# A two-layer four-mixer decoder trunk on one core: norm inputs split from the residual, first blocks of a stage, norm root on two columns, mixer steps respaced, layers written out

## The chip, the core and the metric

One core of one Trainium2 chip runs the whole program. The metric is the device time of one execution in microseconds (us), lower is better. The kernel before takes 1369.31 us (median of 3 runs, 1369.11 to 1370.75).

## What is computed

Two layers run on an input x of 256 tokens by 1024 channels, all in float32. The reference, cut to the skeleton:

```python
def hybrid_layer(x, ...):
    h = x + 0.5 * swiglu(rms_norm(x, ffn1_norm), ffn1_w_in, ffn1_w_out)
    u = rms_norm(h, mix_norm)
    proj = u @ w_in          # q, k, v of two attentions, S5 input, GLA inputs, 4 x 1024 gates
    y_sb, y_s5, y_gla, y_dsa = ...      # four causal mixers, each 256 wide
    mixed = jnp.sum(sigmoid(gates) * einsum(branches, w_branch), axis=2)
    h = h + mixed @ w_out
    return h + 0.5 * swiglu(rms_norm(h, ffn2_norm), ffn2_w_in, ffn2_w_out)
```

`rms_norm` divides by the root of the mean square over the 1024 channels and multiplies by a gain per channel. `swiglu` is 1024 -> 2 x 2816 -> 1024. The four mixers are stick-breaking attention ("sb"), a diagonal complex state-space scan ("s5"), gated linear attention ("gla") and dilated window attention ("dsa").

## The kernel before

**Layout.** Activations lie transposed: the residual `hT` is 128 partitions x 8 channel tiles x 256 tokens. A product with weights is made of three matmuls that replace one in float32: `three` (L418 to L422) multiplies the rounded part `hi` of one side with `hi` and `lo` of the other, and `lo` with `hi`. So each operand is split into `hi` (a rounded copy, by ScalarE) and `lo` (the rest, a subtraction).

**Weights.** They come as a stream of blocks of 128 x 2048 values. SyncE loads block after block into a ring of three slots of `raw`. ScalarE rounds a block in two halves (`round_half`, L744), VectorE subtracts in two halves (`half_rest`, L989), TensorE uses it. A block costs TensorE 48 matmuls of 128x256. VectorE's `rest_of_weights` for block m+3 stands in its program at block m, between the other work of block m.

**Stages.** A layer is FFN 1 (33 blocks), mixer (36 blocks: 11 projections, 16 gates, 4 branches, 5 output blocks) and FFN 2 (33 blocks). All engines run in the order in which their program is written, with semaphores between them, and the two layers are a hardware loop (`Fori`) on each engine.

**Norm.** The gain is applied first and the root last. After a residual pair of tiles q is ready (`hT`, 4 pairs q = 0 to 3), VectorE multiplies it by the gain into `U` (`gain_pair`, L1000), ScalarE rounds `U` (`split_pair`, L755) and squares `hT` (`square_pair`, L759), and GpSimd subtracts for the `lo` part (`split_stream`, L1436). TensorE's first block of the stage waits for `lo` of each pair. VectorE adds the four squares (`add_squares`, L1007 to L1011), TensorE sums over partitions with a matrix of -1 (`sum_squares`, L460), behind the stage's first block, with the result on 256 token columns of all partitions; for the mixer's norm it also makes two columns with the tokens on partitions. Then in `norm`: VectorE scales (L1038), ScalarE takes logarithm and exponential for the root (L789, L790, each with a table load), and VectorE makes one Newton step (L1040 to L1043) on all 256 columns. The root is applied when a product is read from PSUM: `scale` (L1072) in the FFN, `evacuate` (L1380; L874 on ScalarE) in the mixer.

**FFN.** Two input blocks give the two halves of a hidden pair, one output block takes it. `scale`, ScalarE's SiLU (L776), `product` (L1077), `hidden_hi` (L783) and `hidden_lo` (L1082) make the hidden tiles. At the end of an FFN VectorE runs `rest_of_weights`, then for q = 0 to 3 the residual (L1130) and the gain (L1000), then `rest_of_weights`, `add_squares`, and in `last_rest` the third block of weights.

**Mixer.** Its block m is called m in the code (0 "s5u", 1 "sbq", 2 "sbk", 3 "gg", 4 "dq", 5 "dk", 6 "gqk", 7 "sbv", 8 "dv", 9 "gv", 10 "gr", from 11 on the gates). Each engine has a function `pieces(m)` with what it does for the four mixers behind block m; block 3 has 24 matmuls, the others 48. The S5 scan has 8 tiles. Tile i goes through TensorE (`s5_in`), VectorE (`s5_rotate`, L1151 to L1154), GpSimd (L1529, L1530), VectorE (`s5_scan`, L1160), GpSimd (six operations, L1537 to L1543) and TensorE (`s5_out`). VectorE's part of tile i stands at m = i + 1, TensorE's `s5_out` at m = i + 4. The first scan needs GpSimd's tables (`rotations`, made during FFN 1) and `coefficients`, which needs an exponential that ScalarE makes behind the mixer's norm (L793).

The steps of the sb attention are: scores (TensorE), softplus (ScalarE, then VectorE L1202, L1205), suffix sums (`sb_suffix`, TensorE), exponential (ScalarE L884), mask (VectorE L1210), `attend`. Heads 0 and 1 go at m = 3 and 4, heads 2 and 3 at m = 5 and 6, `attend` at m = 8. At m = 7 VectorE makes the arguments of the GLA decays (L1226, L1227, 16 instructions), ScalarE their exponentials (L893, L894), and TensorE makes `gla_scores` at m = 9.

**End.** After the last residual the kernel of before still makes gain, splits, squares and weight halves for a stage that does not come, since the loop body is the same for both layers.

## Time and profile before

| what | value |
| --- | --- |
| median of 3 runs | 1369.31 us |
| the profiled execution, its own time | 1366.64 us |
| its span, first to last instruction | 1364.8 us |
| TensorE matmul busy | 1276.4 us, 94% |
| VectorE busy | 938.4 us, 69% |
| ScalarE busy | 638.8 us, 47% |
| GpSimd busy | 391.0 us, 29% |
| mean granted TensorE clock | 0.971 of full speed |
| DMA | 224.97 MB, mean 165 GB/s |

The busy shares come from one profiled execution. Matmuls are pipelined, so "busy" counts overlapping instructions once; the rate is read from how many matmuls start in a stretch. The profiled execution is 2.67 us shorter than the median of the runs.

### The profile page before, as it was taken

How to read it: one execution, taken by the hardware profiler on the slowest of the kernel's cores; microseconds unless marked ns; L12 is line 12 of the kernel's file. 1: busy time of each engine (PE TensorE's matmuls, PEld its weight loads, DVE VectorE, ACT ScalarE, POOL GpSimd, SP SyncE). 2: the span in 40 equal slices, each digit the busy share in tenths (PEclk: the TensorE clock that was granted, in tenths of full speed). 3: DMA queues.
4: the chain of work that ended last, by engine and by line, in shares of the span. 5: the costliest groups of instructions: out<-in, count | busy, mean ns of one | idle time of the engine just before them, and what ended most of it. 6: DMA issues, size and time to landing. Idle time of an engine off the chain costs nothing. (4 is left out here: it accounts for less than half of the span.)

```text
span 1364.8 us, 26906 instructions
## 1 busy us (share of the span) xinstructions
PE 1276.4 (94%) x10296; PEld 1240.6 (91%) x10296; DVE 938.4 (69%) x1249; ACT 638.8 (47%) x871; POOL 391.0 (29%) x516
## 2 busy tenths in 40 slices
PE   6999999799999899999989999996899998999996
PEld 6999998678999799999979999985799997999996
DVE  6657767778775776555676686676888567655557
ACT  5543445445554454444454434455346444544444
POOL 1389105772001510000015880167610034000001
PEclk9999999798999899999999999998899998999998
DMA  7554544223344355455535445442243543654543
GB/s 284 215 185 156 213 164 146 93 94 125 126 184 168 142 191 196 177 182 184 184 126 189 181 155 214 155 155 93 77 143 125 191 167 135 251 182 178 179 179 114
DMA packets 31478, 224.97 MB, mean 165 GB/s; under 512 B 3616, under 2 KB 3616, under 8 KB 4384
## 3 DMA queue, kind: packets, MB, share of 16 engines
q1 hardware_dynamic: 31392, 223.84, 45.5%
q8 instruction: 52, 0.85, 0.2%
q14 instruction: 34, 0.28, 0.1%
HBM read 222.78 MB, written 1.05 MB: 164 GB/s over the span
## 5 line engine op out<-in xcount | busy, mean ns | idle before, releaser
L989 DVE TENSOR_TENSOR w_lo_t<-raw,w_hi_t 128x1024 fp32r<-128x1024 f32 x414 | 529.8, 1319 | 83.1 <-ACT w_hi_t L744 83.1
L744 ACT ACTIVATE w_hi_t<-raw 128x1024 fp32r<-128x1024 f32 x414 | 414.0, 1046 | 149.2 <-PE banks L422 146.8
L420 PE MATMUL banks<-u_hi_t,w_hi_t 128*128 128x256 f32 x1552 | 449.0, 289 | 30.9 <-DVE w_lo_t L989 13.2
L421 PE MATMUL banks<-u_lo_t,w_hi_t 128*128 128x256 f32 x1552 | 444.0, 286 | 0.0
L422 PE MATMUL banks<-u_hi_t,w_lo_t 128*128 128x256 f32 x1552 | 443.7, 286 | 0.0
L420 PEld LDWEIGHTS banks<-u_hi_t,w_hi_t 128*128 128x128 f32 x1552 | 302.8, 195 | 39.1 <-issue 19.0
L421 PEld LDWEIGHTS banks<-u_lo_t,w_hi_t 128*128 128x128 f32 x1552 | 302.9, 195 | 0.1
L422 PEld LDWEIGHTS banks<-u_hi_t,w_lo_t 128*128 128x128 f32 x1552 | 302.8, 195 | 0.0
L420 PE MATMUL banks<-b_hi_t,w_hi_t 128*128 128x256 f32 x864 | 245.1, 284 | 0.6 <-POOL b_lo_t L1436 0.6
L421 PE MATMUL banks<-b_lo_t,w_hi_t 128*128 128x256 f32 x864 | 244.5, 283 | 0.0
L422 PE MATMUL banks<-b_hi_t,w_lo_t 128*128 128x256 f32 x864 | 244.5, 283 | 0.0
L420 PE MATMUL banks<-h_hi_t,w_hi_t 128*128 128x256 f32 x640 | 183.0, 286 | 8.6 <-DVE h_lo_t L1082 8.6
L421 PE MATMUL banks<-h_lo_t,w_hi_t 128*128 128x256 f32 x640 | 182.6, 285 | 0.0
L422 PE MATMUL banks<-h_hi_t,w_lo_t 128*128 128x256 f32 x640 | 182.4, 285 | 0.0
L1436 POOL TENSOR_TENSOR u_lo_t<-U,u_hi_t 128x512 fp32r<-128x512 f32 x20 | 28.2, 1412 | 526.9 <-ACT u_hi_t L755 526.9
L776 ACT ACTIVATE sbqk<-sbqk 128x256 f32<-128x256 f32 x88 | 36.7, 417 | 280.8 <-DVE sbqk L1072 280.8
L420 PEld LDWEIGHTS banks<-b_hi_t,w_hi_t 128*128 128x128 f32 x864 | 165.9, 192 | 1.0 <-POOL b_lo_t L1436 1.0
L421 PEld LDWEIGHTS banks<-b_lo_t,w_hi_t 128*128 128x128 f32 x864 | 165.9, 192 | 0.1
L422 PEld LDWEIGHTS banks<-b_hi_t,w_lo_t 128*128 128x128 f32 x864 | 165.9, 192 | 0.0
L420 PEld LDWEIGHTS banks<-h_hi_t,w_hi_t 128*128 128x128 f32 x640 | 124.2, 194 | 9.4 <-DVE h_lo_t L1082 9.4
L422 PEld LDWEIGHTS banks<-h_hi_t,w_lo_t 128*128 128x128 f32 x640 | 124.4, 194 | 0.0
L421 PEld LDWEIGHTS banks<-h_lo_t,w_hi_t 128*128 128x128 f32 x640 | 124.3, 194 | 0.0
(218 smaller groups left out, 1415.8 us busy)
## 6 DMA issues: line engine op xcount, KB each, us to landing
raw<-weights SPq DMA_DIRECT2D x207, 1024.0 KB, 4.8
prm<-params SPq DMA_DIRECT2D x2, 1178.5 KB, 5.3
prm<-params SPq DMA_DIRECT2D x1, 1166.5 KB, 15.3
cst<-constants SPq DMA_DIRECT2D x1, 1027.0 KB, 11.5
hT<-x_t SPq DMA_DIRECT2D x2, 512.0 KB, 5.1
out_t<-hT SPq DMA_DIRECT2D x4, 256.0 KB, 2.0
prm<-params SPq DMA_DIRECT2D x1, 12.0 KB, 1.8
```

What stands on the lines that cost most here:

```text
L420: pe.matmul(o, st[0], mv[0], start=start, stop=False, skip_group_check=True)
L421: pe.matmul(o, st[0], mv[1], start=False, stop=False, skip_group_check=True)
L422: ins = pe.matmul(o, st[1], mv[0], start=False, stop=stop, skip_group_check=True)
L744: act.activation(w_hi[:, slot, a:a + HALF], raw[:, slot, a:a + HALF], ACT.Copy) \
L776: act.activation(ab[:, buf, 0, :], ab[:, buf, 0, :], ACT.Silu).then_inc(s.h_silu, 1)
L989: dve.tensor_tensor(w_lo[:, slot, a:a + HALF], raw[:, slot, a:a + HALF], w_hi[:, slot, a:a + HALF].bitcast(F32), ALU.subtract).then_inc(s. ...
L1436: pool.tensor_tensor(in_lo[where][:, 2 * q:2 * q + 2, :], U[:, 2 * q:2 * q + 2, :], in_hi[where][:, 2 * q:2 * q + 2, :].bitcast(F32), ALU. ...
```

## The change

1. **Split from the residual.** `U` is no longer used for the gain. ScalarE writes `hi` as gain times `hT` (two instructions of 128x256 for a pair, the gain as scale), VectorE writes `lo` as gain times `hT` minus `hi` (two instructions of 128x256). GpSimd has no part in it. The squares go to `U`.
2. **End of an FFN.** VectorE's residuals, its splits and the two halves of a weight block alternate.
3. **First two blocks of a stage.** `first_two` runs blocks 0 and 1 one behind the other (the order in turns is there, but switched off), with `sum_squares` between them and a new `rstd_to_row` in the middle of the second. Block 2 of the mixer has a bank of its own (`bank_of`), and does not wait for the reading of block 0.
4. **Norm root on two columns.** `sum_squares` gives 128 tokens on partitions x 2 columns. GpSimd takes the power -1/2 of these 2 columns (`root`), VectorE makes the Newton step on them, and TensorE turns them back into a row over 256 columns on all partitions, which VectorE copies from PSUM. ScalarE's logarithm, exponential and their table loads for the norms go.
5. **Mixer.** The S5 tiles stand one block later on VectorE and TensorE (m = i + 2, `s5_out` at m = i + 5). The exponential that `coefficients` needs is made in FFN 1. The sb suffix sums stand at m = 5 and 8, masks at m = 6 and 9, `attend` and `gla_scores` at m = 10; most later pieces stand one block later.
6. **Layers written out** as Python loops. All waits have constant values, and the last FFN ends with the residuals. The last three weight blocks and the last parameters are not loaded.
7. **Start.** The first weight block is loaded in two halves, between and behind the halves of x.

The diff, cut to its core:

```diff
+TURNS = [(j, q) for q in range(4) for j in range(2)]
+STRAIGHT = [(j, q) for j in range(2) for q in range(4)]
+SS_AFTER, ROW_AFTER = {True: 5, False: 3}, {True: 6, False: 5}
+def bank_of(m):
+    return 2 if m == 2 else m % 2
-        squares = [yb[:, 0, :, :], yb[:, 1, :, :], sbqk[:, 0, :, :], sbqk[:, 1, :, :]]
+        squares = [U[:, 2 * q:2 * q + 2, :] for q in range(4)]
...
             sp.dma_start(hT[:, 0:4, :], x_in[:, 0:4, :]).then_inc(s_x[0], 16)
+            sp.dma_start(raw[:, 0, 0:HALF], stream[0][:, 0:HALF]).then_inc(s_first, 16)
             sp.dma_start(hT[:, 4:8, :], x_in[:, 4:8, :]).then_inc(s_x[1], 16)
-            load(0, 0)
+            sp.dma_start(raw[:, 0, HALF:BLK], stream[0][:, HALF:BLK]).then_inc(landed[0], 16)
...
-            with pe.Fori(0, LAYERS) as layer:
+            for layer in range(LAYERS):
+                def first_two(b, bank, norm, where):
+                    in_turns = False
+                    for n, (j, q) in enumerate(TURNS if in_turns else STRAIGHT):
+                        if q == 0:
+                            block_ready(b + j)
...
+                        pe.wait_ge(s.u_lo, layer * PER.u_lo + 4 * norm + q + 1)
+                        in_part(b + j, (b + j) % 3, bank + j, where, (2 * q, 2 * q + 1))
+                        if n == SS_AFTER[in_turns]:
+                            sum_squares(norm)
+                        if n == ROW_AFTER[in_turns]:
+                            rstd_to_row(norm)
...
+                    for tt in range(2):
+                        for k in range(2):
+                            ins = single(banks[:, 7, tt:tt + 1], squares[0][:, k, tt * P:(tt + 1) * P],
+                                         c("neg_ones")[:, 0:1], tt == 0 and k == 0, k == 1)
+                def rstd_to_row(norm):
+                    pe.wait_ge(s.rstd, layer * PER.rstd + norm + 1)
+                    for tt in range(2):
+                        ins = single(banks[:, 7, T + tt * P:T + (tt + 1) * P], rstd[:, norm, tt:tt + 1].to_broadcast([P, P]),
+                                     c("ident"), tt == 0, True)
+                    ins.then_inc(s.row, 1)
...
+            def split_pair(stage, name, q, where=0):
+                act.wait_ge(s.res, 4 * stage + q + 1)
+                for kt in (2 * q, 2 * q + 1):
+                    ins = act.activation(in_hi[where][:, kt, :], hT[:, kt, :], ACT.Copy, scale=p_(name)[:, kt:kt + 1])
+                ins.then_inc(s.u_hi, 1)
...
-                def norm(n):
-                    width = T + 2 if n == 1 else T
-                    act.wait_ge(s.v, layer * PER.v + n + 1)
-                    own.link(act.activation(n_y[:, 0:width], n_v[:, 0:width], ACT.Ln))
-                    act.activation(n_y[:, 0:width], n_y[:, 0:width], ACT.Exp, scale=-0.5).then_inc(s.y0, 1)
...
+            def split_pair(stage, name, q, where=0):
+                dve.wait_ge(s.u_hi, 4 * stage + q + 1)
+                for kt in (2 * q, 2 * q + 1):
+                    ins = dve.scalar_tensor_tensor(out=in_lo[where][:, kt, :], in0=hT[:, kt, :],
+                                                   scalar=p_(name)[:, kt:kt + 1],
+                                                   in1=in_hi[where][:, kt, :].bitcast(F32),
+                                                   op0=ALU.mult, op1=ALU.subtract)
+                ins.then_inc(s.u_lo, 1)
...
+                    if last:
+                        for q in range(4):
+                            residual(q)
+                        return
+                    rest_of_weights(layer, k0 + i + 1, 0)
+                    residual(0)
+                    half_rest(layer, k0 + i + 1, 1, 0)
+                    split(0)
+                    residual(1)
+                    half_rest(layer, k0 + i + 1, 1, 1)
+                    residual(2)
+                    split(1)
+                    residual(3)
+                    split(2)
+                    split(3)
                     add_squares(layer * 3 + (1 if f == 0 else 3))
+                    rest_of_weights(layer, k0 + i + 1, 2)
...
+                def root(n):
+                    pool.wait_ge(s.v, layer * PER.v + n + 1)
+                    pool.tensor_tensor(nrm[:, 1, :], nrm[:, 0, :], const(4, (P, 2)), ALU.pow).then_inc(s.y0, 1)
```

Three places show how the instructions stand. In the rows, L numbers are lines of the kernel they belong to, and `x2` means twice in a row.

The first is VectorE at the end of FFN 1. Before:

```order
L1130 SCALAR_TENSOR_TENSOR hT<-banks,hT 128x512
L1134 ISA
L1000 TENSOR_SCALAR U<-hT,prm 128x256 x2
L1127 REGISTER_ALU
L1130 SCALAR_TENSOR_TENSOR hT<-banks,hT 128x512
...
L1000 TENSOR_SCALAR U<-hT,prm 128x256 x2
L988 REGISTER_ALU
L989 TENSOR_TENSOR w_lo_t<-raw,w_hi_t 128x1024
L988 REGISTER_ALU
L989 TENSOR_TENSOR w_lo_t<-raw,w_hi_t 128x1024
```

Now:

```order
L1184 SCALAR_TENSOR_TENSOR hT<-banks,hT 128x512
L1033 TENSOR_TENSOR w_lo_t<-raw,w_hi_t 128x1024
L1045 SCALAR_TENSOR_TENSOR u_lo_t<-hT,prm,u_hi_t 128x256 x2
L1184 SCALAR_TENSOR_TENSOR hT<-banks,hT 128x512
L1033 TENSOR_TENSOR w_lo_t<-raw,w_hi_t 128x1024
L1184 SCALAR_TENSOR_TENSOR hT<-banks,hT 128x512
L1045 SCALAR_TENSOR_TENSOR u_lo_t<-hT,prm,u_hi_t 128x256 x2
L1184 SCALAR_TENSOR_TENSOR hT<-banks,hT 128x512
L1045 SCALAR_TENSOR_TENSOR u_lo_t<-hT,prm,u_hi_t 128x256 x4
L1055 TENSOR_TENSOR U<-U 128x512
```

The two weight halves moved from behind the fourth residual to behind the first two, and the `lo` part, which GpSimd made, now stands in VectorE's order.

The second is VectorE in the mixer, at the two sb heads 0 and 1 (`attA`). Before, at m = 3, behind the scan of tile 2:

```order
L989 TENSOR_TENSOR w_lo_t<-raw,w_hi_t 128x1024
L1160 SCALAR_TENSOR_TENSOR s5x<-s5n,s5x 128x256 x2
L1201 ISA
L1202 SCALAR_TENSOR_TENSOR attA<-banks,attB 128x384
L192 REGISTER_ALU
L1205 TENSOR_TENSOR attA<-attA,cst 128x384
```

Now, at m = 4, again behind the scan of tile 2:

```order
L1225 TENSOR_TENSOR s5x<-banks,G 128x256
L1033 TENSOR_TENSOR w_lo_t<-raw,w_hi_t 128x1024 x2
L1231 SCALAR_TENSOR_TENSOR s5x<-s5n,s5x 128x256 x2
L1273 SCALAR_TENSOR_TENSOR attA<-banks,attB 128x384
L1276 TENSOR_TENSOR attA<-attA,cst 128x384
```

The heads still stand behind the scan of tile 2; both moved by one block.

The third is TensorE at the first suffix sums (`attA,cst`). Before, all this stands behind block 4:

```order
L433 MATMUL banks<-s5u,prm 128x256 x2
L433 MATMUL banks<-st,s5c 32x256 x2
L613 REGISTER_ALU
L433 MATMUL banks<-gq,prm 128x256
L563 ISA
L433 MATMUL banks<-attA,cst 128x256
L433 MATMUL banks<-attA,cst 128x128 x2
```

Now, behind block 5:

```order
L438 MATMUL banks<-w_hi_t,u_lo_t 128x256
L449 MATMUL banks<-s5u,prm 128x256 x2
L449 MATMUL banks<-st,s5c 32x256 x2
L449 MATMUL banks<-attA,cst 128x256
L449 MATMUL banks<-attA,cst 128x128 x2
```

There is one block of 48 matmuls more ahead of the wait.

## Rows read from the trace of the kernel before

**Rows 1.** The page, its head and part 1: busy us (share) xinstructions

```profile
span 1364.8 us, 26906 instructions
PE 1276.4 (94%) x10296; PEld 1240.6 (91%) x10296; DVE 938.4 (69%) x1249; ACT 638.8 (47%) x871; POOL 391.0 (29%) x516
```

**Rows 2.** Windows: stretch and its us, busy us (xinstructions), PEclk, DMA share, GB/s

```profile
100.00:150.00 50.00, 50.00 (x419) 50.00 (x418) 39.66 (x35) 21.63 (x30) 37.95 (x40) 1.00 0.45 160
248.00:261.60 13.60, 4.86 (x19) 4.49 (x19) 10.76 (x15) 1.82 (x3) 11.85 (x12) 0.50 0.23 78
507.40:510.80 3.40, 3.40 (x18) 3.40 (x18) 2.96 (x3) 1.32 (x3) 0.00 (x0) 0.50 0.50 207
```

**Rows 3.** Waits of TensorE: who waited <- for whom: us in total, times, longest

```profile
PE banks L433 <- DVE attA L1205: 22.1, 4, 9.3
PE banks L420 <- DVE w_lo_t L989: 13.2, 1, 13.2
PE banks L420 <- DVE u_lo_t L1361: 12.7, 6, 2.7
...
PE banks L420 <- DVE h_lo_t L1082: 8.6, 4, 4.2
PE banks L433 <- DVE yb L1011: 4.3, 5, 1.3
PE banks L420 <- POOL u_lo_t L1436: 3.4, 7, 0.7
```

**Rows 4.** Timeline of the end: start, us, engine line operation; last row: DMA issues

```profile
1352.68 0.28 PE L422 MATMUL banks<-u_hi_t,w_lo_t 128*128 128x256 f32 x1
...
1354.65 0.68 DVE L1130 SCALAR_TENSOR_TENSOR hT<-banks,hT 128x512 f32<-128x512 f32 x1
...
1362.18 2.35 DVE L989 TENSOR_TENSOR w_lo_t<-raw,w_hi_t 128x1024 fp32r<-128x1024 f32 x2
...
out_t<-hT SPq DMA_DIRECT2D x4, 256.0 KB, 2.0
```

**Rows 5.** Timeline of TensorE, end of FFN 1 to second mixer block [idle <- releaser]

```profile
208.26 0.28 PE L422 MATMUL banks<-u_hi_t,w_lo_t 128*128 128x256 f32 x1
...
217.60 0.48 PE L433 MATMUL banks<-yb,cst 128*128 128x256 f32 x1 [1.31 <-DVE yb L1011]
...
225.30 0.48 PE L433 MATMUL banks<-s5u,prm 32*128 32x256 f32 x1
```

**Rows 6.** Timeline from layer 1 to layer 2, TensorE and VectorE

```profile
681.42 0.28 PE L422 MATMUL banks<-u_hi_t,w_lo_t 128*128 128x256 f32 x1
...
695.60 0.43 DVE L1038 TENSOR_SCALAR yb<-banks 128x256 f32<-128x256 f32 x1 [2.27 <-issue]
...
707.91 0.39 PE L420 MATMUL banks<-h_hi_t,w_hi_t 128*128 128x256 f32 x1 [4.16 <-DVE h_lo_t L1082]
```

**Rows 7.** Timeline of the first mixer: TensorE, VectorE, GpSimd

```profile
243.66 0.73 POOL L1529 TENSOR_TENSOR s5x<-s5x 128x256 f32<-128x256 f32 x1
252.71 0.72 POOL L1529 TENSOR_TENSOR s5x<-s5x 128x256 f32<-128x256 f32 x1
...
254.14 1.27 DVE L1160 TENSOR_TENSOR_SCAN s5x<-s5n,s5x 128x256 f32<-128x256 f32 x2 [2.77 <-POOL s5x L1530]
...
256.74 0.79 PE L433 MATMUL banks<-attA,cst 128*128 128x256 f32 x1 [9.29 <-DVE attA L1205]
...
310.37 0.44 PE L433 MATMUL banks<-gq,U 32*128 32x32 f32 x4 [4.53 <-DVE s5x L1154]
...
330.26 0.40 PE L433 MATMUL banks<-st,s5c 128*32 128x256 f32 x1
```

**Rows 8.** Groups by shape, VectorE and GpSimd: busy us, mean ns | idle before

```profile
L1361 DVE SCALAR_TENSOR_TENSOR u_lo_t<-U,u_hi_t 128x256 fp32r<-128x256 f32 x16 | 7.7, 480 | 0.4 <-ACT u_hi_t L960 0.4
...
L1436 POOL TENSOR_TENSOR u_lo_t<-U,u_hi_t 128x512 fp32r<-128x512 f32 x20 | 28.2, 1412 | 526.9 <-ACT u_hi_t L755 526.9
...
L1445 POOL TENSOR_TENSOR s5n<-s5n 128x8 f32<-128x8 f32 x162 | 59.6, 368 | 28.5 <-ACT s5n L793 16.0
```

More of the change, by code:

```diff
@@ L95 @@
     rstd = 3
-    u = 12
+    row = 3
+    row_read = 3
     u_hi = 12
@@ L163 @@
     dve = 62
-    act = 16
+    act = 13
     pool = 216
@@ L289, in build @@
         s.rstd = sem("rstd")
-        s.u = sem("u")
+        s.row = sem("row")
+        s.row_read = sem("row_read")
         s.u_hi = sem("u_hi")
@@ L391, in _ @@
             sp.dma_start(prm[:, NGAIN:NPARAM], params_in[0][:, NGAIN:NPARAM]).then_inc(s_params, 16)
-            with sp.Fori(0, LAYERS) as layer:
+            for layer in range(LAYERS):
                 def next_three(n0):
@@ L433, in single, with in_part @@
                 return pe.matmul(o, st, mv, start=start, stop=stop, skip_group_check=True)
-            with pe.Fori(0, LAYERS) as layer:
+            for layer in range(LAYERS):
                 def block_ready(b):
                     pe.wait_ge(s.w_lo, layer * PER.w_lo + 2 * b + 8)
-                def in_block(b, slot, bank, norm=None, where=0, tiles=2):
-                    block_ready(b)
-                    for kt in range(KT):
-                        if norm is not None:
-                            pe.wait_ge(s.u_lo, layer * PER.u_lo + 4 * norm + kt // 2 + 1)
+                def in_part(b, slot, bank, where, kts, tiles=2):
+                    for kt in kts:
                         for ct in range(tiles):
@@ L448, in in_block @@
                                   act_tiles(kt, where=where), kt == 0 and ct == 0, last, s.w_used if last else None)
+                def in_block(b, slot, bank, where=0, tiles=2):
+                    block_ready(b)
+                    in_part(b, slot, bank, where, range(KT), tiles)
+                def first_two(b, bank, norm, where):
[3 more added lines that the diff above has]
+                            block_ready(b + j)
+                            if in_turns:
+                                pe.wait_ge(s.res, layer * PER.res + 4 * norm + j + 1)
+                        pe.wait_ge(s.u_lo, layer * PER.u_lo + 4 * norm + q + 1)
[4 more added lines that the diff above has]
+                            rstd_to_row(norm)
                 def natural_block(b, slot, bank):
@@ L732, in ffn_steps, with first_block @@
             return (0 if f == 0 else FFN_BLOCKS + MIX_BLOCKS) // RING
+        def first_block(layer, k, slot):
+            return layer == 0 and isinstance(k, int) and k == 0 and slot == 0
         @block.scalar
@@ L1120, in ffn, with residual @@
                     hidden_lo(f, FT - 1, 1, end_hi[f], end_lo[f])
-                    rest_of_weights(layer, k0 + i + 1, 0)
-                    if f == 1:
-                        dve.wait_ge(s_params, (layer + 2) * 16)
-                    for q in range(4):
+                    last = (layer, f) == (LAYERS - 1, 1)
+                    def residual(q):
                         if q < 3:
@@ L1431, in _ @@
         def _(pool):
-            def split_stream(done, where=0):
-                for q in range(4):
-                    pool.wait_ge(s.u_hi, done + q + 1)
-                    pool.tensor_tensor(in_lo[where][:, 2 * q:2 * q + 2, :], U[:, 2 * q:2 * q + 2, :],
-                                       in_hi[where][:, 2 * q:2 * q + 2, :].bitcast(F32), ALU.subtract).then_inc(s.u_lo, 1)
-            split_stream(0)
             pool.wait_ge(s_const, 16)
-            with pool.Fori(0, LAYERS) as layer:
+            for layer in range(LAYERS):
                 own = Steps(pool, s.pool, layer, PER.pool)
@@ L1550, in mix @@
                     pool.tensor_tensor(U[:, dt, :], p[:, 0, :], p[:, 1, :], ALU.add).then_inc(s.mixed, 1)
+                root(0)
                 pool.wait_ge(s_params, (layer + 1) * 16)
                 rotations()
-                split_stream(layer * PER.u_hi + 4)
                 coefficients()
+                root(1)
                 for i in range(ST):
@@ L1559, in _ @@
                     mix(dt)
-                split_stream(layer * PER.u_hi + 8, where=1)
-                split_stream(layer * PER.u_hi + 12)
+                root(2)
                 assert own.n == PER.pool, own.n
```

273 lines of the change are left out of this document (143 added, 130 removed).

## The prediction

> **What bounds the kernel now.** I read the page's head and busy shares first, then windows, TensorE's waits, and the timeline around each long wait. TensorE is busy 94% of the span [rows 1]. In a clean window 419 matmuls start in 50 us, 0.119 us each [rows 2], so a block of 48 costs 5.73 us. All 10296 at that rate would take 1229 us of the 1364.8 us span. The other 136 us are a head of 13.2 us before the first matmul [rows 3], a tail of 12 us behind the last [rows 4], and about 110 us of waits, small matmuls and low clock in between. Steady FFN blocks have nothing to give. What a change can gain is in the head, the tail, the six starts of a stage and the mixer.
>
> The waits of TensorE name the places [rows 3]: sb masks in the mixer (22.1 us), `lo` of the mixed tiles before the output blocks (12.7), `h_lo` at the first output block of an FFN (8.6 in four), the squares' sum (4.3), GpSimd's `lo` (3.4). The granted clock adds to them. Around the longest wait it is 0.50 of full speed, the 1.2 GHz level, for 13.6 us, after TensorE had gone idle; in such a stretch of 3.4 us only 18 matmuls start where 28.5 would at full clock, 1.3 us lost [rows 2].
>
> **Tail, 8.6 us.** The last matmul starts at 1352.68, but the last residual starts only at 1354.65, since VectorE has gains to do first. Behind it come splits, squares and weights that nobody needs, up to 1364.5 [rows 4]. With the residuals alone, the last one starts at about 1353.05 and takes 0.7; the store needs 2.0 to land [rows 4], and the closing barrier some 0.4. That ends the span near 1356.2, so 8.6 us go. This depends on no guess about another engine.
>
> **Mixer norm, 2.9 us per layer, 5.8 in all.** Before, the FFN's last matmul starts at 208.26, and the second mixer block ends at 225.30 [rows 5]: 17.0 us for 96 matmuls worth 11.5, so 5.6 us lost. Now I walk VectorE: residual 0 at 203.9, one weight half 1.2, split 0.9, residual 1, a half, residual 2, split 1 done at 209.9, residual 3, splits 2 and 3 done at 211.4 and 212.4. A split is two instructions of 128x256 with two tensors, 0.48 each on VectorE [rows 8]; ScalarE's two are not in the trace, and I take the same. TensorE waits about 0.7 for the pairs. The squares' sum is ready at 214.7, 0.3 after block 0. Its eight one-column passes cost 0.9, and the two products that make the row 0.6 (estimates from the small matmuls in the same timeline). Together 2.7 lost instead of 5.6. The split gives VectorE 3.8 us more work per stage start and takes away four gain pairs; GpSimd loses 1.41 per pair [rows 8], which no one misses.
>
> The root is the unknown. GpSimd's power on two columns does not occur in the trace. Below it is bounded by nothing better than zero, near it stands 0.37 us for 8 columns, and above 1.41 for 512 [rows 8]. I take 0.4, as the nearest in size. Newton's four steps on two columns cost between 0 and 0.43 each, the time of 256 columns [rows 6]; I take 0.2. Then the root is ready 1.5 us after VectorE's scaling, at 218.5, and TensorE arrives for it at 218.6, after half of block 1. There is no slack: every microsecond more is paid in five of the six norms.
>
> **Layer to layer, 7.9 us.** From 681.42 to 707.91 TensorE runs three blocks, 17.2 us of work in 26.5 [rows 6]; a half-clock stretch behind it adds 1.3. In it lie VectorE's 2.27 at the loop's jump ("issue") and a 4.16 wait for `h_lo` [rows 6]. With layers written out the jump goes. The root comes 7 us earlier, and `h_lo` of the second hidden tile is ready 7.8 us after the first `scale`, about 0.3 before TensorE needs it. What stays is the 2.7 of above: 9.3 + 1.3 - 2.7 = 7.9.
>
> **The other three starts, 7.0 us.** These are the first FFN and FFN 2 in both layers. The `h_lo` waits other than that 4.2 are 8.6 - 4.2 = 4.4 [rows 3], and all go, since the first `scale` comes over 2 us earlier. One has a half-clock stretch, 1.3 [rows 2]. At the very start the second half of block 0 lands as before, behind the same bytes, but only one half is left to round and subtract, 1.1 earlier (a half is 1.2 on VectorE [rows 4]). Smaller waits for the squares and `lo` give 0.8, and the row's product takes back 0.6.
>
> **Mixer, 5.3 us per layer, 10.6 in all.** GpSimd's S5 tiles follow each other every 9.05 us (243.66 to 252.71 [rows 7]), slower than TensorE's 5.7 plus small matmuls. VectorE runs in order, so its scan of tile 2 waits 2.77 for GpSimd until 254.14, and only then come the sb masks, for which TensorE idles 9.29 until 256.74 [rows 7]. The change doesn't remove this order. It starts the tiles earlier, as the coefficients are out of the way: tile 0 at 231.5 instead of 234.5. And it puts one more block ahead of each wait. Walked with the durations of before: scan 2 at 251.1, masks for both heads by 254.8; TensorE arrives at 249.8, waits 3.9 and ends at 256.0 what ended at 260.5 before, with block 5 (5.7 us) done too. The second pair costs a wait of 1.1. Then a new one: the mask of heads 2 and 3 now stands behind the scan of tile 7 at m = 9, where VectorE comes at about 306.0; TensorE reaches `attend` at m = 10 at 299.0 and idles 7.0. It takes the place of the 4.53 before `gla_scores` [rows 7], which now stand behind it. Block 11 ends at 321.0, low clock included, instead of 330.26 [rows 7]; one `s5_out` of 1.1 is still to do. Of 8.2 us, 2.9 are counted already. From there every piece is one block later, the last (branch 3's `lo`) at block 22 of 27, so nothing is late for the branches.
>
> **At nothing.** The wait of 12.7 us before the output blocks [rows 3] is GpSimd's chain of sums, which stays. SyncE's wait for `lo` before the parameters is 1 us later; the blocks behind it have over 10 us until they are rounded.
>
> **Sum.** 8.6 + 5.8 + 7.9 + 7.0 + 10.6 = 39.9 us. The profiled execution took 1366.64 and would take 1326.7; the median of before lies 2.67 above it. Against the median the forecast is 1369.3 - 39.9 = 1329.4, say **1329 us**.
>
> **Rivals.**
>
> *The mixer gains nothing.* The 7 us wait at m = 10 grows by as much as the first shrinks. For it: VectorE reaches m = 9 by a chain over four engines, and tiles later in the mixer follow more slowly than 9.05 apart. Then 10.6 are missing: 1340.
>
> *The mixer gains more.* If VectorE reaches the last mask about 5 us sooner, TensorE's idle and low clock shrink by 8 a layer: 1313. Against it: my walk uses tile periods that were measured.
>
> *The root is dear.* By the rows it may take 1.41, 1.0 more than I took, on the path in five norms: 1334. One still longer costs 5 us for each microsecond. The Trainium skill, in "GPSIMD Engine Reference", section 2.1, says that the first call of a freshly loaded GpSimd routine costs about 6 us with no instruction visible; no row here shows one, and if each norm paid it, this term would be some 28 us and the time near 1357.
>
> *Slower: the respaced mixer waits on GpSimd.* `attend` now needs the scan of tile 7, seven periods behind tile 0; before it needed one some tiles earlier. If the tiles follow each other every 12.5 us instead of 9.05, VectorE comes 24 us later to the mask and TensorE idles that much longer in each layer: 1329 + 48 = 1377. It decides from a period of about 12. Against it: only tiles held up by VectorE or TensorE had such periods.
>
> *Slower: code supply.* Written-out layers could make engines wait for instructions. Such a wait is 2.27 at the loop's jump [rows 6]; 18 of them on TensorE's path cancel the gain, 20 give 1374. Against it: the body of one layer was straight code already, and TensorE's longest waits [rows 3] are all for other engines. The Trainium skill, "Advanced Engine Details and Errata", section "ISA Cache", says that an engine holds two lines of 256 instructions; if each new line stalled TensorE the kernel of before would be full of such gaps, which the rows don't show.
>
> **Chances.** Forecast 0.58 (its own range 1321 to 1336), mixer gains nothing 0.15, more 0.11, dear root 0.10, slower by the mixer 0.04, by code 0.02. Those that end slower hold 0.05 with part of the last, and none lies near no change, since the tail alone is 0.6%: a difference of 0.2%, 2.7 us, is about what can be told. The range takes in the first three rivals' main part, 1314 to 1343.
>
> **What would show it.** Right: a last residual within 1 us of the last matmul and a span ending 3.5 us behind it; no "issue" wait on VectorE between layers; `h_lo` gone from TensorE's waits; the wait for the sb masks split into about 4, 1 and 7 us per layer; GpSimd's power near 0.4 us. Wrong: a wait of TensorE for the root (a product with `cst` behind VectorE's `rstd`) over 0.5 us, an sb wait above 10 us, or "issue" waits on TensorE inside a stage.

## The result and the profile after

The changed kernel takes **1346.8 us** (median of 4 runs, 1345.45 to 1347.22) against 1369.2 before: a ratio of 0.9832, 95% interval 0.9815 to 0.9849. So it is faster, by 22.4 us, where 40 were forecast, and it lies 3.8 us above the stated range (1314 to 1343). The page's head and part 1 of the changed kernel (compare [rows 1]):

```profile
span 1345.1 us, 25665 instructions
PE 1279.2 (95%) x10328; PEld 1246.1 (93%) x10328; DVE 907.2 (67%) x1238; ACT 639.4 (48%) x876; POOL 362.0 (27%) x494
```

The span is 19.7 us shorter than the 1364.8 of before. To see where they come from I count TensorE's matmuls with weights (48 a block, 24 in three short blocks of each mixer) and note when each stage's block starts in either trace:

| TensorE starts | before | changed | difference | since the row above | forecast |
| --- | --- | --- | --- | --- | --- |
| first matmul | 13.25 | 14.06 | +0.81 | +0.8 | |
| layer 1, FFN 1, block 5 | 46.73 | 47.41 | +0.69 | -0.1 | part of -7.0 |
| mixer, m = 0 | 208.03 | 208.69 | +0.67 | 0.0 | 0 |
| m = 2 | 226.36 | 222.47 | -3.89 | -4.6 | -2.9 |
| m = 23 | 407.06 | 407.75 | +0.69 | **+4.6** | **-5.3** |
| FFN 2, block 5 | 520.26 | 517.83 | -2.44 | -3.1 | part of -7.0 |
| layer 2, FFN 1, block 5 | 721.00 | 710.33 | -10.67 | -8.2 | -7.9 |
| mixer, m = 0 | 882.30 | 871.61 | -10.69 | 0.0 | 0 |
| m = 2 | 900.63 | 885.37 | -15.26 | -4.6 | -2.9 |
| m = 23 | 1080.06 | 1070.14 | -9.91 | **+5.3** | **-5.3** |
| FFN 2, block 5 | 1191.52 | 1180.10 | -11.41 | -1.5 | part of -7.0 |
| last matmul | 1352.68 | 1341.26 | -11.41 | 0.0 | 0 |
| end of the span | 1364.8 | 1345.1 | -19.7 | -8.3 | -8.6 |

(About 1.1 us of each gain ahead of m = 2 and of each loss behind it are one thing: `s5_in(0)`, four small matmuls that stood behind m = 1 and now stand behind m = 2.) Most of it went near the forecast, but not the two mixers, which should have given 10.6 us and took 9.9. The waits of TensorE in the changed kernel (who <- for whom: us, times, longest; compare [rows 3]):

```profile
PE banks L449 <- DVE attA L1276: 20.3, 4, 6.1
PE banks L436 <- DVE w_lo_t L1033: 14.1, 1, 14.1
PE banks L436 <- DVE u_lo_t L1433: 13.0, 6, 2.7
PE banks L449 <- issue: 11.8, 5, 5.7
...
PE banks L436 <- DVE h_lo_t L1138: 1.2, 1, 1.2
```

`h_lo` fell from 8.6 to 1.2, GpSimd's `lo` is gone, but the sb masks (L1276) stand at 20.3 where 22.1 stood. The "issue" row is mostly `attend` at m = 10, which waits for the masks of heads 2 and 3: VectorE ends these at 313.45 and TensorE starts at 313.55. Now the timeline of the first of these waits (start, us, engine, line, operation, [idle before <- releaser]):

```profile
252.12 0.72 POOL L1599 TENSOR_TENSOR s5x<-s5x 128x256 f32<-128x256 f32 x1
252.87 1.27 DVE L1231 TENSOR_TENSOR_SCAN s5x<-s5n,s5x 128x256 f32<-128x256 f32 x2 [3.58 <-POOL s5x L1599]
254.06 0.53 DVE L1273 SCALAR_TENSOR_TENSOR attA<-banks,attB 128x384 f32<-128x384 f32 x1
254.63 0.79 DVE L1276 TENSOR_TENSOR attA<-attA,cst 128x384 f32<-128x384 f32 x1
255.47 2.93 PE L449 MATMUL banks<-attA,cst 128*128 128x256 f32 x8 [6.06 <-DVE attA L1276]
```

VectorE idles 3.58 for GpSimd with the scan in front of it, the masks stand behind the scan, and TensorE idles 6.06 for the masks, although what they need from ScalarE was there at 240.1. The other two waits of the layer:

```profile
285.89 1.27 DVE L1231 TENSOR_TENSOR_SCAN s5x<-s5n,s5x 128x256 f32<-128x256 f32 x2 [1.29 <-POOL s5x L1599]
288.49 1.86 PE L449 MATMUL banks<-attA,cst 128*128 128x256 f32 x5 [4.08 <-DVE attA L1276]
310.73 1.28 DVE L1231 TENSOR_TENSOR_SCAN s5x<-s5n,s5x 128x256 f32<-128x256 f32 x2 [1.98 <-POOL s5x L1599]
311.92 1.53 DVE L1281 SCALAR_TENSOR_TENSOR attA<-attA,cst 128x384 f32<-128x384 f32 x2
313.55 2.00 PE L449 MATMUL banks<-attA,sbv 128*64 128x256 f32 x10 [5.51 <-issue]
```

6.1, 4.1 and 5.5 us against the forecast 3.9, 1.1 and 7.0. And the engines hold each other: after its long wait TensorE is late with `s5_out(1)`, GpSimd needs that to free its buffer, and its tile 3 stands still for 5.18 us:

```profile
261.86 0.73 POOL L1599 TENSOR_TENSOR s5x<-s5x 128x256 f32<-128x256 f32 x1
267.77 0.72 POOL L1606 TENSOR_TENSOR s5x<-s5x,G 128x256 f32<-128x256 f32 x1 [5.18 <-PE banks L449]
```

Starts of the eight S5 tiles on GpSimd in the first mixer, and the distance from each to the next:

| kernel | tile 0 | tile 7 | distances |
| --- | --- | --- | --- |
| before | 234.5 | 310.4 | 9.2 9.0 9.7 **13.0** 9.3 11.6 14.1 |
| changed | 231.0 | 309.3 | 11.2 9.2 9.8 **12.9** 9.4 12.3 13.5 |
| old_spacing | 226.4 | 306.9 | 11.0 9.4 9.7 **13.0** 9.2 14.1 14.1 |
| sb_first | 230.7 | 304.5 | 11.2 9.8 9.2 9.3 9.0 11.8 13.5 |
| sb_ahead | 230.9 | 304.1 | 11.2 9.8 9.2 9.3 9.5 11.9 12.3 |

(The last three are runs of below.) The low clock follows the waits. The windows of the changed kernel (stretch, its us, PE, PEld, DVE, ACT, POOL busy (x), PEclk, DMA share, GB/s; compare [rows 2]):

```profile
100.00:150.00 50.00, 50.00 (x419) 50.00 (x418) 39.41 (x36) 25.83 (x33) 45.85 (x55) 1.00 0.47 163
311.60:325.20 13.60, 11.65 (x129) 10.70 (x130) 8.17 (x11) 1.04 (x2) 6.75 (x6) 0.50 0.32 120
```

The wait for `attend` is followed by 13.6 us at 0.50 of full speed, the 1.2 GHz level, which `attend`, the 96 small matmuls of `gla_scores` and the start of block 11 all pay. In the first mixer the half clock lasts 27 us in all, 24 before.

The start of a stage, VectorE at the mixer's norm, with GpSimd and TensorE between:

```profile
217.25 0.15 DVE L1092 TENSOR_SCALAR nrm<-banks 128x2 f32<-128x2 f32 x1
...
217.49 0.71 POOL L1531 TENSOR_TENSOR nrm<-nrm,cst 128x2 f32<-128x2 f32 x1 [61.08 <-DVE nrm L1092]
...
218.23 0.16 DVE L1094 TENSOR_TENSOR nrm<-nrm 128x2 f32<-128x2 f32 x1 [0.82 <-POOL nrm L1531]
...
219.04 0.71 PE L449 MATMUL banks<-cst,rstd 128*128 128x128 f32 x4
...
219.79 0.42 DVE L1099 COPY rstd_row<-banks 128x256 f32<-128x256 f32 x1 [0.80 <-PE banks L449]
```

The root takes 0.71 (0.69 to 0.71 in all six), and TensorE shows no idle time before the row's product. The end of the program (compare [rows 4]):

```profile
1341.26 0.28 PE L438 MATMUL banks<-u_hi_t,w_lo_t 128*128 128x256 f32 x1
1341.58 0.69 DVE L1184 SCALAR_TENSOR_TENSOR hT<-banks,hT 128x512 f32<-128x512 f32 x1 [0.74 <-PE banks L438]
```

### The profile page after: what moved, and what is told of

The parts are those of the page before. It is cut to its first block and busy times, and to the rows that moved or that the text cites. A ratio compares the mean times of both kernels' runs of the same rounds, so it can differ in the third digit from the quotient of the medians.

```text
span 1345.1 us, 25665 instructions
## 1 busy us (share of the span) xinstructions
PE 1279.2 (95%) x10328; PEld 1246.1 (93%) x10328; DVE 907.2 (67%) x1238; ACT 639.4 (48%) x876; POOL 362.0 (27%) x494
## 3 DMA queue, kind: packets, MB, share of 16 engines
HBM read 218.42 MB, written 1.05 MB: 163 GB/s over the span
## 5 line engine op out<-in xcount | busy, mean ns | idle before, releaser
L1033 DVE TENSOR_TENSOR w_lo_t<-raw,w_hi_t 128x1024 fp32r<-128x1024 f32 x408 | 516.2, 1304 | 88.2 <-ACT w_hi_t L789 88.1
L789 ACT ACTIVATE w_hi_t<-raw 128x1024 fp32r<-128x1024 f32 x408 | 408.1, 1046 | 159.9 <-PE banks L438 159.4
L436 PE MATMUL banks<-u_hi_t,w_hi_t 128*128 128x256 f32 x1552 | 450.1, 290 | 27.5 <-DVE w_lo_t L1033 14.1
L1531 POOL TENSOR_TENSOR nrm<-nrm,cst 128x2 f32<-128x2 f32 x6 | 4.2, 698 | 396.2 <-DVE nrm L1092 396.2
## 6 DMA issues: line engine op xcount, KB each, us to landing
out_t<-hT SPq DMA_DIRECT2D x4, 256.0 KB, 2.3
```

Source lines behind the costliest of these rows:

```text
L436: pe.matmul(o, st[0], mv[0], start=start, stop=False, skip_group_check=True)
L789: act.activation(w_hi[:, slot, a:a + HALF], raw[:, slot, a:a + HALF], ACT.Copy) \
L1033: dve.tensor_tensor(w_lo[:, slot, a:a + HALF], raw[:, slot, a:a + HALF], w_hi[:, slot, a:a + HALF].bitcast(F32), ALU.subtract).then_inc(s. ...
L1531: pool.tensor_tensor(nrm[:, 1, :], nrm[:, 0, :], const(4, (P, 2)), ALU.pow).then_inc(s.y0, 1)
```

## The experiments

A ratio is to the kernel before, run on the same chip (median 1366.4 to 1368.9 us); 1346.8 is the changed kernel. Where nothing else is said, a run edits the changed kernel.

**Layers written out, alone** (written_out), in the kernel before, on all five engines:

```diff
-            with dve.Fori(0, LAYERS) as layer:
+            for layer in range(LAYERS):
```

> The kernel before with one part of the change: its two layers as Python loops and not as hardware loops. Theory 1 (as predicted): the 2.27 us of VectorE at the jump between the layers go, they are on the path, some 2 to 3 us: 1366 to 1367, and nowhere else does anything change by over 1 us. Theory 2 (code supply): longer code makes engines wait, 1371 or more. Theory 3: most of the 8.2 us gained between the layers comes from this part: about 1362.

Measured 1365.4 us, ratio 0.9986 (0.9971 to 1.0000): 1 us won, at the edge of what can be told, where theory 1 had 2 to 3, and no sign of theory 2 or 3 in the sum. Block by block, in one profiled execution of each kernel, it is less quiet: 3.8 us are won between the layers and 2.7 in the first mixer and FFN 2, but 2.4 are lost at the first FFN's start, 1.4 in layer 2, and 2.1 in the middle of FFN 1, where nothing was changed:

```profile
141.28 2.02 DVE L1082 TENSOR_TENSOR h_lo_t<-yb,h_hi_t 128x256 fp32r<-128x256 f32 x1 [0.48 <-ACT h_hi_t L783]
```

That subtraction takes 0.42 us elsewhere. Here it falls beside GpSimd's table work for S5, and TensorE waits 1.87 for it. So of the 8.2 us that the whole change wins between the layers nearly half (3.8) come from the loop by this run, where the prediction had its jump at 2.27.

**The root on ScalarE** (root_scalar), on the same two columns:

```diff
-                    pool.tensor_tensor(nrm[:, 1, :], nrm[:, 0, :], const(4, (P, 2)), ALU.pow).then_inc(s.y0, 1)
+                    own.link(act.activation(nrm[:, 1, :], nrm[:, 0, :], ACT.Ln))
+                    act.activation(nrm[:, 1, :], nrm[:, 1, :], ACT.Exp, scale=-0.5).then_inc(s.y0, 1)
```

> The changed kernel with the norms' root made by ScalarE on the same two columns, by logarithm and exponential with their table loads, and not by GpSimd's power. GpSimd's takes 0.97 us from VectorE's scaling to its first Newton step; ScalarE's should take about 3.2 (two loads of 1.28, two short functions). If the root is on the path in every norm: 2.2 more in each of six, and 1.28 for the load of the SiLU behind it in the four of an FFN, less where VectorE's weights hide it: about 1346.8 + 15 = 1362, with TensorE waiting in the middle of a stage's second block. If the root is hidden by the second block: within 3 us of 1346.8.

Measured 1351.5, ratio 0.9883 (0.9861 to 0.9906): 4.7 us dearer. ScalarE had loaded the logarithm's table ahead of the wait in five of six norms, so the root took 2.0 us where GpSimd's took 0.8, and TensorE now waits for it in all six:

```profile
DVE nrm L1103 <- ACT nrm L827: 12.1, 6, 3.1
...
PE banks L449 <- DVE rstd L1106: 5.4, 6, 1.2
```

1.2 us more in each, 1.0 paid in each from the second norm on: there is no slack behind the root, as the prediction had it.

**The end of an FFN as before** (end_order), on VectorE:

```diff
-                    residual(0)
-                    half_rest(layer, k0 + i + 1, 1, 0)
-                    split(0)
-                    residual(1)
-                    half_rest(layer, k0 + i + 1, 1, 1)
-                    residual(2)
-                    split(1)
-                    residual(3)
-                    split(2)
-                    split(3)
+                    for q in range(4):
+                        residual(q)
+                        split(q)
+                    rest_of_weights(layer, k0 + i + 1, 1)
```

> The changed kernel with VectorE's order at the end of an FFN as before: the four residuals, each with its split, and then the two halves of the weight block, and not these halves between the first residuals. Theory 1 (the alternation is part of the gain): the pairs come sooner (residual and split 1.6 us a pair instead of up to 2.8), but the second block's weights some 2.5 us later and with them the squares' sum and the root: TensorE, which needs the second block 6 us after the first, waits under 1 us: within 2 us of 1346.8 in all three starts. Theory 2 (as in the kernel before, where the sum stood behind the halves): the root comes 2.4 us later and is paid in three norms: 1353.

Measured 1362.0, ratio 0.9958 (0.9940 to 0.9976): 15 us lost, more than either theory allowed. Each of the three starts behind an FFN takes 5.3 us longer; from m = 0 to m = 2 of the mixer it is 19.0 us, more than the 18.3 of the kernel before. VectorE's timeline shows what both theories left out:

```profile
205.36 0.69 DVE L1184 SCALAR_TENSOR_TENSOR hT<-banks,hT 128x512 f32<-128x512 f32 x1 [1.81 <-PE banks L438]
207.11 0.88 DVE L1045 SCALAR_TENSOR_TENSOR u_lo_t<-hT,prm,u_hi_t 128x256 fp32r<-128x256 f32 x2 [1.06 <-ACT u_hi_t L801]
```

A split right behind its residual waits 1.05 to 1.06 us for ScalarE to make `hi`, four times in a row. The alternation of residuals, weight halves and splits covers that. Without it block 0 of the mixer and the squares' sum behind it take 11.3 instead of 7.4 us. Of these 3.9 us, 1.4 are TensorE's waits for the late pairs. The other 2.3 are theory 2's mechanism at another place: the adding of the squares, now behind the splits and the two halves, ends at 219.8 instead of 215.1, and TensorE waits 2.55 us for it where it waited 0.21. Behind these waits the clock falls (0.66 of full speed on the mean from 221 to 226), which costs another 1.4; for the root itself TensorE does not wait. Without the alternation the split from the residual would have won nothing at the mixer's start.

**The mixer at its old positions** (old_spacing), all pieces, with the rest of the change kept (three tables of positions; VectorE's first rows shown):

```diff
-                    if 2 <= m < 2 + ST:
-                        s5_scan(m - 2)
-                    if m in (4, 7):
+                    if 1 <= m <= ST:
+                        s5_scan(m - 1)
+                    if m in (3, 5):
```

> The changed kernel with the mixer's pieces at the positions of the kernel before on TensorE, VectorE and ScalarE (tile i at m = i + 1, s5_out at m = i + 4, sb masks at m = 3 to 6, attend at m = 8, gla_scores at m = 9); all else as changed. Theory 1, a ring: from the first S5 tile to the eighth TensorE, VectorE and GpSimd hold each other up, some 79 us from tile 0 to tile 7 in both kernels, and the respacing only puts tile 0 a block later. Then tile 0 starts about 6 us sooner than in the changed kernel (225 instead of 231.0), tile 7 too (303 instead of 309.3), and the kernel takes about 1346.8 - 2 x 5 = 1337. Theory 2, as predicted: the respacing by itself gains some 5 us a layer, and what is missing was lost elsewhere; then the old positions cost 10 us: 1357. Between the two, 1343 to 1350: the position of the pieces does not matter.

Measured **1330.7**, ratio 0.9733 (0.9710 to 0.9755): undoing the respacing wins 16 us. (By the profiled spans, 1334.0 against 1345.1, it is 11; its runs go from 1329.7 to 1335.8.) Tile 0 starts 4.6 us sooner, tile 7 2.4 us, and the distances are much the same. The respacing is what the change loses by, and theory 1 has the direction right. But it expected both tiles 6 us sooner and 10 us in all, so the start of the tiles alone does not explain the size. The other difference is where the masks stand. Those for `attend` are here behind the scan of tile 5 and not of tile 7, and TensorE's waits for the sb masks are 14.1 us where they were 20.3. From m = 2 to m = 23 the two mixers now gain 1.3 and 2.4 us over the kernel before instead of losing 4.6 and 5.3.

**Only the S5 tiles at their old positions** (tiles_only), on TensorE and VectorE:

```diff
-                        if 2 <= m < 2 + ST:
-                            s5_rotate(m - 2)
+                        if 1 <= m <= ST:
+                            s5_rotate(m - 1)
```

> The changed kernel with one part of the respacing undone: the S5 tiles stand where they stood before (tile i at m = i + 1, s5_out at m = i + 4), the sb steps, attend and the later pieces stay where the change put them. So the sb masks of m = 4 stand behind the scan of tile 3, those of m = 7 behind tile 6, those of m = 9 behind tile 8's place, which is empty. Theory 1 (the start of the tiles sets the mixer): tile 0 starts at 226.4 as with all old positions, and about 8 us are won over the two layers: 1339. Theory 2 (what counts is how many tiles stand ahead of a mask): TensorE's wait at m = 5 grows by the 5 us that tile 3 is behind tile 2, less the 4.6 of the earlier start, and the time stays within 3 us of 1346.8.

Measured 1340.8, ratio 0.9813 (0.9782 to 0.9845): 6 us of the 16 by the median. Two of its six runs took 1345.0 and 1346.6, and the interval takes in the ratio of the changed kernel (0.9832), so the times alone do not tell the two apart; the profiled executions lie 6.3 us apart. The tiles start 6 us sooner, but one more of them stands ahead of each mask, and TensorE still waits 21.0 us for the sb masks in four. Each theory names one half of that.

**The sb masks ahead of the scan** (sb_first), in the changed kernel:

```diff
                 def pieces(m):
-                    if 2 <= m < 2 + ST:
-                        s5_scan(m - 2)
                     if m in (4, 7):
...
+                    if 2 <= m < 2 + ST:
+                        s5_scan(m - 2)
                     if m == 6:
```

> The changed kernel with one thing moved: in VectorE's pieces the sb masks (m = 4, 6, 7, 9) stand ahead of the scan of that block's S5 tile and not behind it. Theory 1 (the order on VectorE makes the waits): TensorE's waits for the sb masks, 20.3 us in four, fall under 4 us; GpSimd's wait of 5.2 us for s5_out at tile 3 goes with them, and the tiles follow each other at about 9.5 us. Tile 7 starts some 7 us sooner and the kernel takes about 1346.8 - 2 x 7 = 1333. Theory 2 (the tiles' own rate sets the mixer): the waits go over to s5_out or attend, and the time stays within 3 us of 1346.8.

Measured 1331.9, ratio 0.9725 (0.9699 to 0.9751): theory 1's time. The wait at m = 5 goes (block and pieces take 11.0 instead of 17.5 us), and so does GpSimd's 5.2 at tile 3: the distance 12.9 becomes 9.3. The waits for the masks do not fall under 4 us, though; at m = 8 4.5 us a layer are left:

```profile
PE banks L449 <- DVE attA L1274: 11.0, 4, 4.5
```

**Both together** (old_sb_first): old positions, masks ahead of the scan.

> Both earlier edits together: the mixer's pieces at the positions of the kernel before, and on VectorE the sb masks of a block ahead of the scan of that block's S5 tile. Alone, the first took 16 us off the changed kernel and the second 15. Theory 1 (both remove the same wait, VectorE's masks behind a tile, once by starting the tiles sooner and once by not standing behind them): no more than 5 us beyond either, 1326 to 1331. Theory 2 (two separate losses, one the late start of the tiles and the other the order on VectorE): they add up, 1346.8 - 31 = 1316.

1323.6, ratio 0.9672 (0.9650 to 0.9695): between the theories, 7 to 8 us beyond either. What waits now is `gla_scores` at m = 9, for the rotation of tile 7, 8.9 us at the longest.

**The masks of m = 7 and 9 ahead of rotation and weights too** (sb_ahead; `masks` holds the four groups of masks):

```diff
                     for m in range(NPROJ + NGATE):
+                        if m in (7, 9):
+                            masks(m)
                         if not BY_ACT[m]:
```

> As the run with the sb masks ahead of the scan (1331.9), and at m = 7 and m = 9 they also stand ahead of VectorE's rotation of the tile and its two weight halves. There TensorE still waits 4.5 us (masks of m = 7) and 5.2 us (attend, masks of m = 9) in each layer, with 6.8 and 13.6 us of half clock behind them. Theory 1 (the wait is for VectorE's order alone): VectorE reaches the masks 4 to 5 us sooner, both waits fall under 1 us and most of the half clock goes: 9 + 3 us a layer, 1332 - 24 = 1308. Theory 2 (the tiles are next in line): the waits go over to gla_scores, which need tile 7's rotation, and at most 3 us a layer are won: 1326.

1323.9, ratio 0.9677 (0.9656 to 0.9699): 8 of the hoped 24 us. The waits for the masks are gone (2.7 in four), but a new one stands in their place, for ScalarE, which stands behind VectorE's decays:

```profile
PE banks L436 <- ACT dv L922: 11.2, 2, 5.6
...
PE banks L449 <- DVE attA L1274: 2.7, 4, 1.0
```

**GpSimd's tile cut from eight instructions to six** (short_tile). The two products with `rotC` are left out, so y of S5 is made from other numbers:

```diff
-                    own.mark(pool.tensor_tensor(x[:, 0, 0, :], x[:, 1, 0, :], rotC[:, i, :], ALU.mult))
-                    own.mark(pool.tensor_tensor(x[:, 0, 1, :], x[:, 1, 1, :], rotC[:, i, :], ALU.mult))
```

> The changed kernel with GpSimd's work per S5 tile cut from eight instructions to six: the two products with rotC behind the scan are left out, so y of S5 is made from other numbers. It asks whether GpSimd's time per tile sets the mixer. Theory 1 (a ring in which every tile waits for GpSimd's chain): 1.5 to 2.4 us less per tile, the scan of tile 2 comes 3 to 5 us sooner and tile 7 10 to 15 us sooner, as far as TensorE follows; the time falls by 12 to 20 us, to about 1331. Theory 2 (TensorE and VectorE's weights set the rate, GpSimd only shows the wait): less than 4 us.

1326.5, ratio 0.9695 (0.9673 to 0.9717): 20 us, at the upper end of theory 1. Less work on an engine that is busy 27% of the span shortens the kernel by as much as that: in the mixer it is a link of the ring. TensorE's waits for the sb masks fall from 20.3 to 9.4 us. The distance from tile 3 to tile 4 does not shrink, it grows to 15.0, since GpSimd, done sooner, now waits 6.9 us for `s5_out`.

**SiLU's table loaded first** (early_table):

```diff
             act.wait_ge(s_gain, 16)
+            act.activation(dms[:, 1, 0:8], prm[:, 0:8], ACT.Silu)
             split_pair(0, "g_ffn1", 0)
```

> The changed kernel with one small SiLU of eight columns as ScalarE's first instruction, as soon as the gains are there, so that its table is loaded before x arrives. In the changed kernel a load of 1.28 us stands at 6.05 behind the wait for x, and another at 27.30 in front of the first SiLU. Theory 1: both are on TensorE's path: the first matmul comes at 12.8 instead of 14.06 and block 5 some 2 to 2.6 us sooner, 1344.5. Theory 2: the first block of weights lands as before and hides the first load, and 1.3 us at most are won: 1345.7.

1343.4, ratio 0.9817 (0.9795 to 0.9839): theory 1 and a little more. The interval overlaps that of the changed kernel; that the gain is real rests on the trace. ScalarE at the start, changed kernel:

```profile
6.05 1.28 ACT L801 ACT_TABLE_LOAD   x1 [6.05 <-DVEq L1062]
7.34 1.71 ACT L801 ACTIVATE u_hi_t<-hT,prm 128x256 fp32r<-128x256 f32 x4
...
27.30 1.28 ACT L826 ACT_TABLE_LOAD   x1 [8.06 <-DVE sbqk L1128]
```

and here, with block 5 of FFN 1 starting 2.7 us sooner:

```profile
0.74 1.28 ACT L809 ACT_TABLE_LOAD   x1 [0.74 <-PEq L1763]
...
6.00 1.70 ACT L801 ACTIVATE u_hi_t<-hT,prm 128x256 fp32r<-128x256 f32 x4 [3.25 <-DVEq L1063]
```

**A faster version** (combo): masks ahead, table first, and ScalarE's exponential of the decays behind the reading of dv:

```diff
-                    if m == 7:
+                    if m == 8:
                         act.wait_ge(s.gla_arg, layer * PER.gla_arg + 1)
```

> A version meant to be faster: the run with the sb masks ahead of rotation and weights (1323.9), plus the early table (3.3 us in its own run), plus one ScalarE step moved: the exponential of the GLA decays stands behind the reading of block 8 (dv) and its rounding, and not ahead of them. In the run of 1323.9 TensorE waits 5.6 us a layer for that reading, since ScalarE stands 18 us behind VectorE's decays. Theory 1 (order on ScalarE): the wait goes with some low clock, 6 to 8 us a layer: 1323.9 - 3.3 - 13 = 1308. Theory 2 (gla_scores are next in line, and their input now comes later): the wait moves to m = 10, and only the table's 3 us and 1 or 2 us more are won: 1319.

**1320.4 us** (1315.3 to 1320.8), ratio 0.9642 (0.9613 to 0.9672), the lowest time of all, by 3.2 us, though its interval overlaps those of the next two: the time of theory 2. The wait for dv (5.6) is gone and a longer one at m = 10 has come, 7.5 us, but not ahead of `gla_scores`: it is `attend` that waits, for the masks of m = 9. They end at 298.9, since in VectorE's order the scan of tile 6 and the products for `gla_scores` (293.7 to 296.9) stand ahead of them.

**The same with the tiles at their old positions** (combo_tiles):

> The version above with the S5 tiles where they stood before the change (tile i at m = i + 1, s5_out at m = i + 4). The masks no longer stand behind a scan, so only the start of the tiles is left of the respacing. Theory 1 (start of the tiles counts): tile 7 is 4 to 5 us earlier, gla_scores and attend wait less: 3 to 5 us a layer better than the version above. Theory 2: TensorE reaches s5_out a block sooner than GpSimd's 9 us per tile allows, and waits for s5_state instead; the two versions agree within 3 us.

1326.6, ratio 0.9698 (0.9671 to 0.9726): 6 us slower, against both theories, although tile 7 starts at 292.2 instead of 300.3. TensorE's block m = 10 with its pieces takes 23.6 us instead of 20.4, with 8.5 us of waiting ahead of `attend` where it was 7.5, at half clock for 17.1 us. Why stays open.

## Why the prediction was wrong

By its own terms, per place:

- **Tail, 8.6:** right, 8.3.
- **Mixer norm, 5.8:** 9.1, of which 2.1 are the moved `s5_in`; 7.0. The walk of VectorE was right within half a microsecond (splits done at 212.8, forecast 212.4). **Root:** 0.71 where I took 0.4, ready at 219.0 where 218.5 was forecast, and still nothing paid. "No slack" was right.
- **Layer to layer, 7.9:** right, 8.2.
- **The other three starts, 7.0:** 3.9 net. The two of FFN 2 gave 3.1 and 1.5. The first FFN, where I counted a gain from the half block, lost 0.7. The failed step is "only one half is left, 1.1 earlier": in the kernel before ScalarE loaded its table at 0.74, while x was on its way; now its first function waits for x, and the load of 1.28 stands behind that wait. Another 1.28 stands ahead of the first SiLU, since the logarithm that was followed by that load is gone. The run with the early table gives 3.4 back.
- **Mixer, 10.6:** the failed term. It took 9.9, or 7.8 without the moved `s5_in`: 18.4 us off, nearly the whole miss.

The mixer's step fails in two places. The first is the walk behind scan 2. Set against the first mixer:

| the walk | forecast | measured |
| --- | --- | --- |
| tile 0 starts on GpSimd | 231.5 | 231.0 |
| scan of tile 2 starts | 251.1 | 252.9 |
| first wait of TensorE, and its end | 3.9, 253.7 | 6.1, 255.5 |
| suffix sums behind it end | 256.0 | 259.2 |
| second wait | 1.1 | 4.1 |
| TensorE reaches `attend` | 299.0 | 308.0 |
| last masks done | 306.0 | 313.5 |
| block 11 ends | 321.0 | 329.2 |

The third wait is even shorter than forecast (5.5 against 7.0); what failed is when the engines get there. Scan and masks take 2.7 us, so the forecast had the scan of tile 7 at about 303.3, 72 us behind tile 0. In the kernel before these are 79.2 us (234.5 to 313.7), now 79.7 (231.0 to 310.7): the walk took some 7 us out of the ring, and the change took out none. Where they should have come from the prediction does not show; at 9.05 us a tile, seven distances would be 63 us, and they are 76 before and 78 now. That distance holds for tiles 0 to 3 of the kernel before alone. In the changed kernel already the first is 11.2 us, since four of tile 0's eight operations on GpSimd take 1.6 to 1.8 us where two did before. And the distance behind tile 3 is 13.0 in the kernel before too, 12.9 now. GpSimd waits for `s5_out`, TensorE is late with it since it waited for the masks, and the masks are late since VectorE waited for GpSimd. Kernel before:

```profile
269.02 0.73 POOL L1537 TENSOR_TENSOR s5x<-s5x,G 128x256 f32<-128x256 f32 x1 [5.17 <-PE banks L433]
```

That wait of 5.17 us is 5.18 in the changed kernel. With the masks out of the ring (sb_first) the 13 becomes 9.3.

A smaller error is the clock: the twelve matmuls of the first suffix sums take 3.78 us behind their wait, before and now, and the forecast had 2.3; in the kernel before the same twelve for heads 2 and 3, at full clock, take 2.20.

The second place is "it puts one more block ahead of each wait" as if that were a gain by itself. The tiles were put a block later with everything else, so a ring that starts later ends later, and TensorE fills with that block the time which it would have idled at its start. Of the 8 us by which the coefficients' earlier end could have advanced tile 0 (226.4 at the old positions against 234.5), the change keeps 3.5. A smaller part: behind m = 11 the changed mixer waits 0.8 us for VectorE's dilated weights (0.2 before) and block 11 takes 8.5 us instead of 6.9, since the half clock behind `attend` reaches into it.

Of the rivals, "the mixer gains nothing" named the right place and the right doubt, that later tiles follow more slowly, but was priced at 1340: it let the term go to nought and not below. That the respacing alone could lose was only thought of as a tile distance of 12 us on all tiles, far off in the other direction. The dear root did not come: six powers of 0.70. The Trainium skill, "GPSIMD Engine Reference", section 2.1, gives some 6 us for the first call of a freshly loaded routine; between VectorE's scaling and the first power lie 0.31 us here (22.72 to 23.03), so no such cost is seen. Code supply did not come either.

The change without its respacing takes 1330.7, near the forecast of 1329. That is partly chance: there the mixers gain 3.7 us over the kernel before, not 10.6, and its profiled execution is 5 us slower than its median.

## What to carry to other kernels

When engines pass work round, measure the whole ring from its first piece to its last in the trace of before, every distance, and ask of the longest one what it waits for; a rate read from the first pieces is too good. Moving all of a ring's pieces later by a block buys nothing; what buys is to take out of an in-order engine's way the short instruction that another engine waits for, and to start the ring sooner. Between an instruction and the one that needs another engine's answer to it, put work that needs no answer.

## What the runs showed of the hardware

GpSimd's additions and products of 128x256 come mostly in two durations. Of the 128 on S5's tiles in the changed kernel 70 take under 0.8 us, 34 take 1.6 to 1.8 and 24 lie between. Of the time of the 34, 80% lies beside VectorE's weight subtraction, of that of the 70, 4%. One such line, all its executions, minimum, median, maximum in ns:

```profile
L1610 POOL TENSOR_TENSOR st<-s5x,G x16: 720/929/1712, 238.9 to 978.3; 128x256 f32<-128x256 f32 x16
```

VectorE pays too: the same subtraction of a half takes 1.22 us where GpSimd is idle, 1.76 in about half the cases beside an S5 tile (18 of 32), and up to 3.42 beside the table work of FFN 1. By group, VectorE in the mixer's stretch from 225 to 320 us and in FFN 2, from 500 to 680 (busy us, mean ns | idle before):

```profile
L1033 DVE TENSOR_TENSOR w_lo_t<-raw,w_hi_t 128x1024 fp32r<-128x1024 f32 x20 | 28.4, 1461 | 2.2 <-ACT w_hi_t L789 2.2
L1033 DVE TENSOR_TENSOR w_lo_t<-raw,w_hi_t 128x1024 fp32r<-128x1024 f32 x64 | 75.6, 1222 | 15.7 <-ACT w_hi_t L789 15.7
```

The Trainium skill, "SBUF — State Buffer", section "SBUF: two separate sides", says that a VectorE instruction with two inputs in SBUF and a GpSimd instruction take turns on a shared pair of ports, each blocked while the other runs. The durations agree: an operation of 0.73 that meets a subtraction of 1.22 takes about 1.0 longer. So VectorE's weights lengthen the very chain that VectorE then waits for, by up to 1 us for each GpSimd operation that meets one. This was not varied by itself.
